# Low-query score products of the two key chunks on the two row halves of TensorE's array

## The reference, cut to what matters

```python
logits = jnp.einsum('gnqhd,gnkhd->gnhqk', qb, kb, preferred_element_type=jnp.float32) * ATTN_SCALE
logits = jnp.where(valid[None, :, None], logits + bias[None, None], -jnp.inf)
```

## Time and profile before

| what | us |
|---|---|
| median of 3 runs | 1904.16 |
| lowest and highest run | 1899.39, 1905.26 |
| profiled execution, its span (no other time of its own is given) | 1894.1 |
| from the span to the median | 10.1 |
| the weave, first to last score matmul | 337.1 to 759.4 |

### The profile page before, as it was taken

How to read it: one execution, slowest core, us unless ns; L and a number is a source line. 1 busy time by engine, 2 the same in 40 slices (tenths; PEclk the granted TensorE clock), 3 DMA queues, 4 the chain that set the end, 5 groups by cost and what they waited for, 6 DMA issues and landing times.

```text
span 1894.1 us, 33632 instructions
## 1 busy us (share of the span) xinstructions
PE 1829.2 (97%) x12772; PEld 1690.4 (89%) x12772; DVE 1416.5 (75%) x1911; ACT 897.7 (47%) x1674; POOL 1064.7 (56%) x863
## 2 busy tenths in 40 slices
PE   8999999999999999999989999999999999999999
PEld 7999999888888889865557799999999999999999
DVE  5788830698888767589887564897776778787876
ACT  5434412677777778556652022343333344444442
POOL 4588740677756766334433222355555567787774
PEclk9999999999999999899999999999999999999999
DMA  5344442744455443799966434215334366444432
GB/s 185 143 170 169 177 148 75 156 119 123 101 134 122 123 124 90 249 335 328 319 223 219 180 105 179 91 50 201 147 126 165 148 252 234 159 140 145 148 137 92
DMA packets 139097, 309.31 MB, mean 163 GB/s; under 512 B 31659, under 2 KB 65323, under 8 KB 135228
## 3 DMA queue, kind: packets, MB, share of 16 engines
q1 hardware_dynamic: 115356, 271.15, 43.0%
q10 hardware_dynamic: 23584, 36.04, 5.7%
HBM read 222.42 MB, written 93.28 MB: 167 GB/s over the span
## 4 chain that ended last, share of the span: by engine, by line
PE 71%; DVE 14%; issue 6%; DMA 4%; ACT 3%; POOL 2%; SPq 0%; DVEq 0%; ACTq 0%; POOLq 0%
PE ff_ps L2705 31%; PE proj_ps L467 9%; PE dense_ps L1018 6%; PE wo_psa L2540 5%; PE proj_ps L541 4%; PE att_t_ps L1050 2%; PE wo_psb L2672 2%; DVE silu_half L1179 2%; DMA tmp_xbc<-silu_half 1%; PE wo_psa L2672 1%; PE att_s_ps L1036 1%; PE att_s_ps L1037 1%; DVE att_p L1132 1%; PE ssd_in L1736 1%; PE att_pv_ps L1067 1%
## 5 line engine op out<-in xcount | busy, mean ns | idle before, releaser
L2705 PE MATMUL ff_ps<-ff_set,ff_wring 128*128 128x264 f32 x5376 | 661.9, 286 | 9.3 <-DVE ff_set L3318 3.5
L2705 PEld LDWEIGHTS ff_ps<-ff_set,ff_wring 128*128 128x128 f32 x5376 | 658.9, 189 | 11.9 <-DVE ff_set L3318 3.9
L2374 POOL TENSOR_TENSOR ff_wring<-const,ff_wring 128x256 fp32r<-128x256 f32 (+1 forms) x192 | 212.5, 1110 | 147.3 <-ACT ff_wring L2871 147.2
L948 POOL TENSOR_SCALAR att_p<-att_p,att_rden 128x128 f32<-128x128 f32 (+6 forms) x112 | 195.9, 1758 | 118.2 <-DVE att_rden L1110 118.1
L2871 ACT ACTIVATE ff_wring<-const 128x256 fp32r<-128x256 f32 (+1 forms) x192 | 93.6, 489 | 222.8 <-PE ff_ps L2705 115.4
L3340 DVE TENSOR_TENSOR h<-h,ff_ps 128x528 f32<-128x528 f32 x192 | 133.3, 700 | 52.1 <-PE ff_ps L2705 47.5
L1245 ACT ACTIVATE att_pThi<-att_t_ps 128x512 fp32r<-128x512 f32 x192 | 93.3, 487 | 93.1 <-PE att_t_ps L1050 79.4
L1018 PE MATMUL dense_ps<-u_hi,w_hi 128*128 128x352 f32 x480 | 121.9, 335 | 4.6 <-POOL w_lo L254 2.1
L1132 DVE CUSTOM_DVE_ANT_0 att_p<-att_s_ps,att_bias 128x128 f32<-128x128 f32 (+7 forms) x128 | 95.0, 753 | 38.5 <-PE att_s_ps L1037 35.1
L1018 PE MATMUL dense_ps<-u_hi,w_lo 128*128 128x352 f32 x480 | 119.4, 330 | 0.0
L1018 PE MATMUL dense_ps<-u_lo,w_hi 128*128 128x352 f32 x480 | 119.1, 329 | 0.0
(11 more groups left out here) (367 smaller groups left out, 4357.7 us busy)
## 6 DMA issues: line engine op xcount, KB each, us to landing
tmp_r_sets<-h SPq DMA_DIRECT2D x16, 1848.0 KB, 6.5
ff_setraw<-tmp_r_sets SPq DMA_DIRECT2D x56, 528.0 KB, 5.3
sa_k<-in_cache_k SPq DMA_DIRECT2D x32, 640.0 KB, 8.7
sa_v<-in_cache_v SPq DMA_DIRECT2D x40, 512.0 KB, 4.6
w_raw<-in_w_feat SPq DMA_DIRECT2D x36, 512.0 KB, 6.3
out_qk<-proj_out SPq DMA_DIRECT2D x16, 528.0 KB, 8.0
tmp_bias_rows<-tmp_table ACTq DMA_DIRECT2D x8, 1024.0 KB
att_bias<-tmp_bias_rows SPq DMA_DIRECT2D x16, 512.0 KB, 3.6
```

The source lines that it names most:

```text
L948: pool.tensor_scalar(slot(h, qt), slot(h, qt), rden[:, qt, :], None, ALU.mult).then_inc(normed, 1)
L2374: pool.tensor_tensor(w_set(n)[:, 1], operand(q, m), w_set(n)[:, 0].bitcast(F32), ALU.subtract).then_inc(fw_split, 1)
L2705: mm = pe.matmul(ff_ps[:, (b + g) * 512:(b + g) * 512 + HG], ws[:, wi, k, :], xs[:, xi, k, g * HG:(g + 1) * HG], start=(opens and k == 0 a ...
```

## The change

In tiles 4 to 7 the low-query products use 64 rows each: that of keys 0 to 511 the rows 0 to 63, that of keys 512 to 1023 the rows 64 to 127. For this the keys 512 to 1023 are loaded with halves exchanged (their high part lies in rows 64 to 127), and `q_low` holds the low part in both halves for the queries 512 to 1023. All high products of a tile are issued before its low products. Tiles 0 to 3 keep their 128-row products. The planner's price of tiles 4 to 7 falls. A head has six loads for four and nine casts for eight.

```diff
-        return t + sum(0.117 * (qt + 1) for _, qt in score.get(n, ()))
+        return t + sum(0.0585 * (qt + 1 + min(qt + 1, HALF)) for _, qt in score.get(n, ()))
...
             def load_qk(h):
                 f, r = h // 2, h % 2 * HD
                 if h >= 1:
-                    sp.wait_ge(qk_cast, 8 * h)
-                for buf, first in ((k_raw, D + f * P + r), (q_raw, f * P + r)):
-                    sp.dma_start(buf[0:HD, :], dram["qk"][first:first + HD, 0:SEQ]).then_inc(qk_loaded, 16)
-                    sp.dma_start(buf[HD:P, :], dram["qk_low"][first:first + HD, :]).then_inc(qk_loaded, 16)
+                    sp.wait_ge(qk_cast, 9 * h)
+                first = D + f * P + r
+                for part in range(2):
+                    whole, rest = slice(part * HD, (part + 1) * HD), slice((1 - part) * HD, (2 - part) * HD)
+                    sp.dma_start(k_raw[whole, columns(part)], dram["qk"][first:first + HD, columns(part)]).then_inc(qk_loaded, 16)
+                    sp.dma_start(k_raw[rest, columns(part)], dram["qk_low"][first:first + HD, columns(part)]).then_inc(qk_loaded, 16)
+                first = f * P + r
+                sp.dma_start(q_raw[0:HD, :], dram["qk"][first:first + HD, 0:SEQ]).then_inc(qk_loaded, 16)
+                sp.dma_start(q_raw[HD:P, :], dram["qk_low"][first:first + HD, :]).then_inc(qk_loaded, 16)
...
-            pool.memset(q_low[HD:P, :].bitcast(F32), 0.0).then_inc(padded, 1)
+            pool.memset(q_low[HD:P, columns(0)].bitcast(F32), 0.0).then_inc(padded, 1)
...
                 if qt in (0, NT - 1):
-                    pe.wait_ge(qk_cast, 8 * h + (4 if qt == 0 else 8))
+                    pe.wait_ge(qk_cast, 9 * h + (4 if qt == 0 else 9))
...
                 for c in range(0, w, 512):
                     cw = min(512, w - c)
-                    out = s_ps[:, base + c:base + c + cw]
-                    pe.matmul(out, q_high[:, qt * P:w], k_two[:, c:c + cw], start=True, stop=False)
-                    mm = pe.matmul(out, q_low[:, qt * P:w], k_two[:, c:c + cw], start=False, stop=True)
+                    pe.matmul(s_ps[:, base + c:base + c + cw], q_high[:, qt * P:w], k_two[:, c:c + cw], start=True, stop=False)
+                for c in range(0, w, 512):
+                    cw = min(512, w - c)
+                    rows = slice(0, P) if qt < HALF else slice(c // 512 * HD, (c // 512 + 1) * HD)
+                    mm = pe.matmul(s_ps[:, base + c:base + c + cw], q_low[rows, qt * P:w], k_two[rows, c:c + cw],
+                                   start=False, stop=True)
...
-                    act.wait_ge(qk_loaded, 64 * (h + 1))
+                    act.wait_ge(qk_loaded, 96 * (h + 1))
...
-                act.activation(q_low[0:HD, cols], q_raw[HD:P, cols], ACT.Copy).then_inc(qk_cast, 1)
+                for r in range(part + 1):
+                    act.activation(q_low[r * HD:(r + 1) * HD, cols], q_raw[HD:P, cols], ACT.Copy).then_inc(qk_cast, 1)
```

More of the change, by code:

```diff
@@ L892, in slot, with columns @@
             return probs[:, first:first + (qt + 1) * P]
+        def columns(part):
+            return slice(part * 512, (part + 1) * 512)
         def sample(buf):
@@ L1245, in keep_high @@
                 act.activation(p_hi[:, n % TURNED, off:512], t_ps[n % 2][:, off:512], ACT.Copy).then_inc(hi_kept, 1)
-            def columns(part):
-                return slice(part * 512, (part + 1) * 512)
             def cast_k(h, part):
```

## The result

The changed kernel takes 1918.05 us (median of 4 runs, 1916.3 to 1918.61); the kernel before 1901.95 beside it. The ratio is 1.0078, 95% interval 1.0054 to 1.0102: slower, by 14.8 us (10 to 19). The forecast was 1918.

A forecast was written before the change was run, and what follows sets the result against it. The prediction took TensorE to bound the weave, alone in its last third and with interruptions before. Tiles +14.6, waits -3, start +1.5 and cast +0.5 gave +13.6 us, from 1904.16 to about 1918 us, range 1903 to 1928.

The forecast's parts named there:

- The tiles: TensorE, score tiles 4 to 7: from 3.12 to 4.03 us per head, +14.6 us over 16 heads.
- The way in and out: TensorE, switching to row halves and back: 0.41 us per visit, read from 32-row products in the earlier trace.
- B: Rival, tiles 4 to 7: the halves switch but don't overlap, 1927 us; chance 0.12.
- D: Rival, TensorE's array: no switch and no overlap, only start and casts add 2 to 3 us, 1907; chance 0.08.
- C: Rival, tiles 4 to 7: no switching cost for fp32r, and the halves overlap, 1897 us; chance 0.10.
- What the waits take back: TensorE's waits in the weave's first two thirds: they shrink and hide 3 us, bounds 0 and 9.1.
- E: Rival, heads up to 600 us: waits hide the longer tiles there, 1911 us in all; chance 0.10.
- The ninth cast: ScalarE, tick 4: 0.63 us more per head, mostly hidden, +0.5 us in all, bounds 0 and 4.
- The planner: Placing of dense units under the lower price: 0 us, bounds -2 and +3.
- The start: Chain of loads and casts at the weave's start: two more issues and one more cast, +1.5 us, bounds 0 and 1.9.
- Per-head loads, memset: Two extra load issues per head on SyncE and the halved GpSimd memset: 0 us each.
- The sum: Whole kernel: +14.6 - 3 + 1.5 + 0.5 = +13.6 us, about 1918.

The follow-up runs named there:

- e5_one_low: The changed kernel without the low product of keys 512 to 1023 in tiles 4 to 7; weave 438.1 us, ratio to the kernel before 1.0059.
- e12: The changed kernel with the planner's price of before and some query casts moved to earlier ticks; weave 430.9 us, ratio to the kernel before 1.0048.
- e11: The kernel before with three of a head's eight casts moved to ticks 9 to 11, the rest over ticks 1 to 4; weave 420.8 us, ratio 1.0001.
- e10: The kernel before with only the ninth cast added, plus the half memset and counts that go with it; weave 426.6 us, ratio 1.0042.
- e9: The changed kernel with low products on all 128 rows, the planner's old price and four loads per head, ninth cast kept; weave 426.4 us, ratio 1.0035.
- e2: The changed kernel with low products on all 128 rows and the planner's price of before; weave 426.6 us, ratio to the kernel before 1.0036.
- e1: The changed kernel with the low products of tiles 4 to 7 on all 128 rows; weave 430.3 us, ratio to the kernel before 1.0040.

## Why the prediction was right, point by point

**The tiles:** right. 3.12 to 4.03 us per head was forecast; the trace has 0.88 us more instead of 0.91, and 14.0 instead of 14.6 us in all. The way in and out, read at a 32-row visit of another stage, held for 64 rows and fp32r to some 0.02 us per visit. Rivals B and D are ruled out by the timeline and e5_one_low. C, which the 64-column product of the earlier trace rows spoke for, was wrong: a product on half of the columns in fp32r pays nothing on either side, one on half of the rows does.

**What the waits take back:** mis-sized, 3 us forecast, 8.4 measured (bounds 0 to 9.1), with the cast in place; about 5.5 with the cast out of the way (10.1 of the 14.0 showed in e12 over e11, 1.6 of them the clock's). I counted 12.9 us in waits and thought them too few to meet the tiles. In the early heads they took 7.5 of 8.8 us. E had the mechanism; what made its total wrong is the next two terms.

**The ninth cast:** mis-sized, 0.5 forecast, 4.4 measured (bounds 0 to 4; e10 is just outside). I took ScalarE's share of the windows, an average; in the kernel before it idles on average for 0.05 to 0.5 us in each of the ticks 1 to 7 (between the first transposes of one and the next), and for 0.8 to 1.3 in the others. The path named, through the high part of the probabilities, was the right one, and takes 2.3 us.

**The clock:** not in the sum. I read 1.00 in both windows and carried it over; the changed kernel falls to 0.50 at 359.3 us, right behind the wait for the dense weight, for some 1.6 us, and this lies within the cast's 4.4. The line against E calls the waits "at most 1.4 us long", but the earlier trace rows has this one with 2.1.

**The planner:** 0 forecast, 3.7 measured in the weave, above the bound of +3 (the ratios of the runs give 0.8 with full rows and 3.2 with the halves, neither clear of noise). The text named the likely cause, dense units leaving ticks where VectorE then has less cover, and priced it at nothing.

**The start:** 1.5 forecast. From the first load's issue to the first transposes it is 27.28 us before and 29.03 after, 1.75, of which the cast alone makes 0.80 (28.08 in e10). About 0.5 us of it comes ahead of the first score product, the rest lies in the 13.7 of the weave and can't be told apart from the cast's term.

**Per-head loads, memset:** 0 forecast; e9 against e2 has 0.2.

**The sum:** +13.6 forecast, +13.7 in the weave, +14.8 in the runs. Measured step by step, from before over e9, e2 and e1 to the changed kernel: 4.2 + 0.2 + 3.7 + 5.6 = 13.7. That the total came out right is luck: the halves' net cost was overestimated (11.6 for 5.6) and the rest underestimated (2.0 with the start, for 8.1), and the two errors cancelled. What was understood is the tiles, 14.0 us for 14.6. And the 10.1 us from span to median, of which only 1.9 lies around a span, did no harm since I forecast a difference.

No version here beats the kernel before; e11_early_casts equals it.

## What to carry to other kernels

Running two half-height products side by side pays only if what it saves in one visit is more than the way in and out, 0.41 us here; otherwise leave them on all rows. Gathering many of them in one visit wasn't tried. Before adding a short instruction to an engine that is "73% busy", look at whether it has a pause on the very ticks where the instruction goes. When several engines take turns, don't add up the parts of a change one by one: the waits they share hide the first of them and not the next, so measure them by undoing one at a time. And look at the granted clock of short windows before explaining 2 us: over 265 us a stretch at half speed shows only as 0.99 for 1.00.

## What the runs showed that I had not expected

In fp32r a 64-column product between 128-column ones has a plain step, 0.23 us, while 64 rows cost 0.09 to 0.10 us on each side and an exposed load of 0.11 each. A cast of 0.63 us once in 28 us, on an engine busy for three quarters, came with a stage longer by 4.4 us, all of it in the first eight heads, where 1.5 is the clock; moving three such casts out of the same ticks gave back 1.4. TensorE fell to 1.2 GHz for 3.4 us in eleven of fourteen kernels, just behind a wait of about 2 us, and the kernel before, with the same wait, didn't. And a planner told the measured costs placed the work no better than one told a rougher price.
